# Feed-forward's first product: all of it by Strassen's scheme, in two passes of 768 tokens

## The reference, cut to what matters

```python
def trunk(x, ...):
    mix = token_mixer(rms_norm(x, ln1_pre_g), ...)          # attention and DeltaNet mixers
    x = x + rms_norm(mix, ln1_post_g)
    hid = jnp.square(jax.nn.relu(rms_norm(x, ln2_pre_g) @ w_ff_in))   # (T,1024) @ (1024,4096)
    return x + rms_norm(hid @ w_ff_out, ln2_post_g)
```

## Time and profile before

| | us |
|---|---|
| runs shown (3): median, lowest, highest | 2766.1, 2765.39, 2768.83 |
| the profiled execution, its own time | 2763.01 |
| its span, from the first to the last instruction | 2761.2 |
| PE busy in the span | 2525.7 (91%) |
| `ff_in`, from its first DMA issue to the end of its last product | 1677.2 to 2200.2 |
| the same, from the end of the first pair's part | 1751 to 2200 |

### The profile page before, as it was taken

The page is one execution under the profiler, slowest core; times in us unless marked ns, Lnnn a source line. Parts: engine busy times, 40 slices in busy tenths (PEclk is TensorE's granted clock), DMA queues, the critical chain, the costliest instruction groups (busy, mean ns, idle before and its releaser), DMA issues. The chain is left out here.

```text
span 2761.2 us, 33798 instructions
## 1 busy us (share of the span) xinstructions
PE 2525.7 (91%) x12600; PEld 2106.7 (76%) x12600; DVE 1312.7 (48%) x1700; ACT 890.0 (32%) x1437; POOL 533.8 (19%) x475
## 2 busy tenths in 40 slices
PE   6999999898989979996596993999999889999998
PEld 5888888787979977774485882788888768887887
DVE  5665225256555428886643434644344352234332
ACT  4333323262111117785200332322222141133221
POOL 3352236330111100001420332211121000000000
PEclk9999999999999999998698996999999999999999
DMA  4233212586556551332555444322322273345442
GB/s 136 73 92 88 78 54 102 180 253 215 167 177 186 172 171 70 136 116 74 191 167 180 165 163 150 96 81 88 99 81 85 78 249 112 109 160 201 158 156 103
DMA packets 310734, 373.40 MB, mean 135 GB/s; under 512 B 55760, under 2 KB 237136, under 8 KB 306000
## 3 DMA queue, kind: packets, MB, share of 16 engines
q1 hardware_dynamic: 219712, 294.50, 33.6%
q10 hardware_dynamic: 90896, 77.18, 8.5%
HBM read 251.98 MB, written 119.64 MB: 135 GB/s over the span
## 5 line engine op out<-in xcount | busy, mean ns | idle before, releaser
L2476 PE MATMUL y_ps<-w_hi,hid_hi 128*128 128x512 f32 x768 | 301.1, 392 | 24.4 <-DVE w_lo L2560 16.7
L2476 PE MATMUL y_ps<-w_lo,hid_hi 128*128 128x512 f32 x768 | 300.0, 391 | 0.0
L2476 PE MATMUL y_ps<-w_hi,hid_lo 128*128 128x512 f32 x768 | 299.7, 390 | 0.0
L2566 DVE TENSOR_TENSOR hid_lo<-ff_raw,hid_hi 128x1024 fp32r<-128x1024 f32 x96 | 113.9, 1223 | 319.2 <-ACT hid_hi L2530 319.1
L2530 ACT ACTIVATE hid_hi<-ff_raw 128x1024 fp32r<-128x1024 f32 x96 | 97.3, 1054 | 355.7 <-PE y_ps L2476 329.1
L2117 PE MATMUL ff_ps<-ffx_sums,w_ops 128*128 128x512 f32 x768 | 179.4, 393 | 13.7 <-DVE ffx_sums L2252 13.7
L2476 PEld LDWEIGHTS y_ps<-w_hi,hid_hi 128*128 128x128 f32 x768 | 144.9, 189 | 57.7 <-DVE w_lo L2560 18.2
L2117 PE MATMUL ff_ps<-ffx_rest,w_ops 128*128 128x512 f32 x768 | 181.5, 392 | 8.1 <-DVE ffx_rest L2252 8.1
L2117 PEld LDWEIGHTS ff_ps<-ffx_sums,w_ops 128*128 128x128 f32 x768 | 145.5, 190 | 45.1 <-issue 14.8
L2117 PEld LDWEIGHTS ff_ps<-ffx_rest,w_ops 128*128 128x128 f32 x768 | 145.7, 190 | 38.9 <-issue 8.5
L115 PE MATMUL proj_ps<-ht_hi,win_hi 128*128 128x512 f32 x576 | 173.0, 408 | 0.0
(11 more groups left out here) (255 smaller groups left out, 4885.9 us busy)
## 6 DMA issues: line engine op xcount, KB each, us to landing
ff_raw<-s_hid_s SPq DMA_DIRECT2D x96, 512.0 KB, 4.4
arena<-s_dn_s SPq DMA_DIRECT2D x24, 1024.0 KB, 5.7
s_hid_s<-ff_outs SPq DMA_DIRECT2D x96, 256.0 KB, 2.3
w_raw<-in_w_ff_in SPq DMA_DIRECT2D x16, 1024.0 KB, 5.6
ff_raw<-in_w_ff_out SPq DMA_DIRECT2D x32, 512.0 KB, 4.8
win_raw<-in_w_in SPq DMA_DIRECT2D x27, 512.0 KB, 3.6
s_made_s<-arena SPq DMA_DIRECT2D x12, 1024.0 KB, 4.7
arena<-s_made_s SPq DMA_DIRECT2D x48, 256.0 KB, 6.4
```

Of the source, the lines that this page charges most:

```text
L2476: mm = pe.matmul(acc[:, bank(u, t)], x[:, (t if opens(t) else kh), k], y[:, w], start=w == 0 and first == 0, stop=w == KF - 1 and first == 2)
L2566: dve.tensor_tensor(hlo[:, b, ks].rearrange("p k j -> p (k j)"), raw[:, r], f32(hhi[:, b, ks]).rearrange("p k j -> p (k j)"), ALU.subtract ...
```

## The change

The 1536 tokens are split into two passes of 768, and each pass into two halves of 384 (`WIDE`). In each pass all 16 pairs of weight tiles are gone through, so that there are 32 units (`UNITS`), each of seven products of 12 matmuls with 384 columns; the plain remainder is gone. The weights are loaded, summed and split once for each pass, twice in all. `w1_raw` and `w1_sums` have two buffers each; unit x uses buffer x % 2. All four token sums are made on DVE. C11 is rectified and squared on DVE; C22, C21 and C12 on ACT, in two instructions each.

In `after`, the lines are: loads L2058 (weights) and L2067 (tokens), stores L2085; ACT high parts L2125, token high parts L2135, ReLU L2139, square L2141, copy of P1 L2152; DVE low parts L2168, token low parts L2173, token sums L2183, C11 L2211, its ReLU and square L2214, U2 L2219, U4 L2224, U3 L2228, C22 L2231, C21 L2233, C12 L2238.

```diff
 def ff_in(nc, io):
-        raw = c.sb("w1_raw", [P, KD, 2 * P])
-        sums = c.sb("w1_sums", [P, 4, HK, P])
+    PASSES = 2
+    UNITS = PASSES * PAIRS
+    WIDE = TOK // (2 * PASSES)
+        raw = c.sb("w1_raw", [P, 2, KD, 2 * P])
+        sums = c.sb("w1_sums", [P, 2, 4, HK, P])
...
             @block.sync
+                def load_weights(x):
+                    if x >= 2:
+                        sp.wait_ge(s["w_lo"], 7 * (x - 1))
+                    i = x % PAIRS
+                    sp.dma_start(raw[:, x % 2], ...).then_inc(w_in[x % 2], 16)
...
+                load_weights(0)
+                load_tokens(0)
+                load_weights(1)
+                for x in range(UNITS):
+                    p, i = divmod(x, PAIRS)
+                    if i == 1 and p + 1 < PASSES:
+                        load_tokens(p + 1)
+                    for o in (C11, C22, C21, C12):
+                        if o == C12 and x + 2 < UNITS:
+                            load_weights(x + 2)
+                        if o == C11:
+                            sp.wait_ge(s["curved"], x + 1)
+                        else:
+                            sp.wait_ge(s["squared"], 3 * x + o)
+                        sp.dma_start(io["hid_s"][...], outs[:, o]...).then_inc(out_stored[o], 16)
...
             @block.tensor
+                for x in range(UNITS):
+                    for q in range(7):
+                        if 7 * x + q >= 8:
+                            pe.wait_ge(*used(*divmod(7 * x + q - 8, 7)))
+                        pe.wait_ge(s["w_lo"], 7 * x + q + 1)
+                        if i == 0:
+                            pe.wait_ge(s["x_lo"], 7 * p + q + 1)
...
             @block.scalar
+                for x in range(UNITS):
+                    done(act, x, P1)
+                    act.activation(p1[:], bank(x, P1), ACT.Copy).then_inc(s["p1_done"], 1)
+                    for q in range(7):
+                        if more:
+                            high(x + 1, q)
+                            if i == 0:
+                                prep(p, q)
+                        if q == P7:
+                            relu2(x, C22, "c22_made")
+                            relu2(x, C21, "c21_made")
+                    relu2(x, C12, "c12_made")
...
             @block.vector
+                def following(x, q):
+                    if x + 1 < UNITS:
+                        low(x + 1, q)
+                        if (x + 1) % PAIRS == 0:
+                            prep((x + 1) // PAIRS, q)
...
+                    dve.tensor_tensor(outs[:, C11], p1[:], bank(x, P2), ALU.add).then_inc(s["c11_made"], 1)
+                    following(x, P1)
...
+                    dve.tensor_tensor(outs[:, C21], u2[:], bank(x, P4), ALU.subtract).then_inc(s["c21_made"], 1)
+                    following(x, P4)
+                    following(x, P7)
...
+                    following(x, P3)
+                    if p + 1 < PASSES and i in (4, 6, 8, 10):
+                        token_sum(p + 1, (i - 4) // 2)
```

More of the change, by code:

```diff
@@ L2000, in ff_in @@
     HK = KD // 2
[L2001 to L2005, removed]
+    C11, C22, C21, C12 = range(4)
     with ExitStack() as ctx:
         c = Core(nc, ctx, "ff_in")
[L2008 to L2012, removed]
-        raw = c.sb("w1_raw", [P, KD, 2 * P])
-        w_ops = c.sb("w1_ops", [P, 8, 2, HK, P], F32R)
-        sums = c.sb("w1_sums", [P, 4, HK, P])
[L2016 to L2019, removed]
+        front = c.sb("ffx_raw", [P, 8, HK, WIDE])
+        x_ops = c.sb("ffx_ops", [P, 7, 2, HK, WIDE], F32R)
+        raw = c.sb("w1_raw", [P, 2, KD, 2 * P])
+        w_ops = c.sb("w1_ops", [P, 7, 2, HK, P], F32R)
+        sums = c.sb("w1_sums", [P, 2, 4, HK, P])
+        p1 = c.sb("p1", [P, WIDE])
+        u2 = c.sb("u2", [P, WIDE])
+        u4 = c.sb("u4", [P, WIDE])
+        outs = c.sb("ff_outs", [P, 4, WIDE])
@@ L2067, in prep_views @@
[L2067 to L2075, removed]
+        w_in = [c.sem(f"w_in{u}") for u in range(2)]
@@ new lines, in ff_in, with part_of @@
+        out_stored = [c.sem(f"out_stored{u}") for u in range(4)]
+        r21, r22, r11, r12, t4f, t3f, t1f, t2f = (front[:, n].rearrange("p k t -> p (k t)") for n in range(8))
+        QUADRANT = {0: (0, 0), 1: (1, 0), 2: (0, 1), 3: (1, 1)}
+        SOURCE = {B11: r11, B21: r21, B22: r22, T1: t1f, T2: t2f, T3: t3f, T4: t4f}
+        ARRIVES = {B11: 0, B21: 1, B22: 3}
+        SUMMED = {T1: 0, T2: 1, T3: 2, T4: 3}
+        def part_of(x, op):
+            i, kh = {A11: (0, 0), A12: (0, 1), "A21": (1, 0), A22: (1, 1)}[op]
+            return raw[:, x % 2, kh * HK:(kh + 1) * HK, i * P:(i + 1) * P]
@@ new lines, in _ @@
+                load_weights(0)
+                load_tokens(0)
[9 more added lines that the diff above has]
+                            sp.wait_ge(s["curved"], x + 1)
+                        else:
+                            sp.wait_ge(s["squared"], 3 * x + o)
+                        tile, half = {C11: (0, 0), C22: (1, 1), C21: (1, 0), C12: (0, 1)}[o]
+                        t0 = (p * 2 + half) * WIDE // P
+                        sp.dma_start(io["hid_s"][t0:t0 + WIDE // P, :, 2 * i + tile].rearrange("t p j -> p t j"),
+                                     outs[:, o].rearrange("p (t j) -> p t j", j=P)).then_inc(out_stored[o], 16)
@@ L2112, in _ @@
+                for o in range(4):
+                    sp.wait_ge(out_stored[o], 16 * UNITS)
             @block.tensor
             def _(pe):
[L2115 to L2123, removed]
@@ L2137, in remainder @@
[L2137 to L2140, removed]
-                        for k in range(HK):
[L2142 to L2145, removed]
@@ L2174, in _, with done, out_free, flat @@
+            def done(eng, x, q):
+                eng.wait_ge(s["product"], 7 * x + q + 1)
+            def out_free(eng, x, o):
+                if x:
+                    eng.wait_ge(out_stored[o], 16 * x)
+            def flat(a):
+                return a.rearrange("p k t -> p (k t)")
             @block.scalar
             def _(act):
-                def high(i, op):
-                    operand_ready(act, i, op)
-                    act.activation(w_ops[:, op, 0], source(op), ACT.Copy).then_inc(s["w_hi"], 1)
@@ L2195, in relu2 @@
-                def relu2(i, o, q):
-                    done(act, i, q)
-                    out_free(act, i, o)
-                    dst = outs[:, slot(i, o)]
-                    act.activation(dst, bank(i, q), ACT.Relu).then_inc(s["r_out"], 1)
-                    act.wait_ge(s["r_out"], 2 * i + (o == O_R1) + 1)
-                    act.activation(dst, dst, ACT.Square).then_inc(s["squared"], 1)
-                high(0, A11)
-                for n in range(HK):
-                    prep(n)
-                high(0, A12)
@@ new lines, in prep, with relu2 @@
+                def prep(p, q):
+                    of = RIGHT[q]
+                    if of in ARRIVES:
+                        act.wait_ge(x_in[ARRIVES[of]], 16 * (p + 1))
+                    else:
+                        act.wait_ge(s["t_made"], 4 * p + SUMMED[of] + 1)
+                    if p:
+                        done(act, p * PAIRS - 1, q)
+                    act.activation(flat(x_ops[:, of, 0]), SOURCE[of], ACT.Copy).then_inc(s["x_hi"], 1)
+                def relu2(x, o, made):
+                    act.wait_ge(s[made], x + 1)
+                    act.activation(outs[:, o], outs[:, o], ACT.Relu).then_inc(s["rectified"], 1)
+                    act.wait_ge(s["rectified"], 3 * x + o)
+                    act.activation(outs[:, o], outs[:, o], ACT.Square).then_inc(s["squared"], 1)
@@ new lines, in _ @@
+                for q in range(7):
+                    high(0, q)
+                    prep(0, q)
+                for x in range(UNITS):
+                    p, i = divmod(x + 1, PAIRS)
+                    more = x + 1 < UNITS
+                    done(act, x, P1)
+                    if x:
+                        act.wait_ge(s["u2_done"], x)
+                    act.activation(p1[:], bank(x, P1), ACT.Copy).then_inc(s["p1_done"], 1)
+                    for q in range(7):
+                        if more:
[6 more added lines that the diff above has]
+                    relu2(x, C12, "c12_made")
@@ new lines, in token_sum @@
+                def token_sum(p, n):
+                    dst, a, b, need = ((t1f, r12, r11, (0, 2)), (t2f, r22, t1f, (3,)), (t3f, r22, r12, ()), (t4f, t2f, r21, (1,)))[n]
+                    for m in need:
+                        dve.wait_ge(x_in[m], 16 * (p + 1))
+                    if p:
+                        dve.wait_ge(s["x_lo"], 7 * p)
+                    if n in (1, 3):
+                        dve.wait_ge(s["t_made"], 4 * p + (1 if n == 1 else 2))
+                    dve.tensor_tensor(dst, a, b, ALU.subtract).then_inc(s["t_made"], 1)
@@ new lines, in following @@
+                def following(x, q):
[3 more added lines that the diff above has]
```

(11 more changed lines are left out.)

313 lines of the change are left out of this document (87 added, 226 removed).

## The result

| | before | with the change |
|---|---|---|
| median of 4 runs | 2765.94 us (2765.39 to 2768.83) | 2841.93 us (2836.40 to 2843.77) |
| profiled execution | 2763.0 us | 2842.19 us |
| its span | 2761.2 us | 2840.4 us |
| PE's last product of the stage ends | 2200.2 us | 2275.6 us |

The ratio is 1.0269, with an interval of 1.0251 to 1.0287: 76 us slower, where 50 were forecast. The time is 26 us above the one predicted, inside the range.

What follows compares the result with a forecast made beforehand. A closed ring without PE, 17.1 us a round against PE's 14.56, bounds the stage: 1730 + 496 (29 rounds) + 6.7 + 17.6 ends PE at 2250 against 2200.2, +50 us, so 2816 us; range 2795 to 2850.

Steps and rivals of the forecast that it cites:

- The ring: Closed loop of weights load, DVE and ACT work up to C21's store, next load; without PE, 17.1 us a round.
- landing to C21: From a weights load's landing to the end of C21 on DVE: 9.34 us.
- to C21's square: From the landing through ACT's rectifying and squaring of C22 and C21: 10.94 us.
- to the load's issue: From the landing until SP has issued C21's store and the next load: 11.38 us.
- Issue to landing: Weights load from its issue on SP until it lands: 5.75 us taken, from a range of 5.5 to 6.6.
- My upper bound: Slowest weights landing allowed for, 6.6 us, which makes a round of 18.0 us.
- the beginning: Stage start, DVE the bound on token and weight preparation: load of unit 2 lands at 1730, uncertain by 5 us.
- Narrow matmuls: PE's 384-column matmuls: 0.173 us each forecast; rival had them cost 0.227 like wide ones, +110 us, 2876; 4%.
- The change of pass: One round mid-stage where four low parts of tokens stand ahead of C21 on DVE: 6.7 us longer.
- The rival on the other side: PE stays the bound, the round falling under 14.56 us: PE ends at 2171, 29 us less, 2737; 10%.
- DVE and POOL: Shared SBUF port: POOL gives way by 0.45 us; by the skill's full-block rule the round would be about 17.6.
- The clock: PE's granted clock in the stage: stays 1.00 despite two waits of about 1.2 us a round; nothing charged.

Runs made afterwards that it cites:

- Experiment 1: Changed kernel with the load for unit x+2 issued at the head of unit x's turn on SP, ahead of C11's store: 2737.31 us, 0.9913 of the kernel before.
- experiment 5: Changed kernel with the third of three matmuls per contraction slice (low weights by high tokens) left out in this stage: 2830.69 us.
- experiment 2: Changed kernel with POOL's four sums cut to one column of each 128 from unit 2 on, load left in place: 2746.1 us.
- experiment 3: Changed kernel with the load issued once C21 is squared, ahead of the stores of C22 and C21: 2824.99 us.

## Why the prediction was right, and where a term was off

**The ring was right, link by link.** The prediction's landing to C21 was 9.34, measured 9.39; to C21's square 10.94, measured 11.01; to the load's issue 11.38, measured 11.45. All three were put together from instructions of 512 columns and their spacing. (The text there gives 0.4 for the issue of C21's store, its total holds 0.44, and 0.44 was measured; by the same terms the shortest round is 16.9, not 16.8.) Experiment 1 opens the ring and the loss is gone; experiment 5 takes a third from PE and the loss stays; experiment 2 shortens a link by 3.27 us and the round shortens by as much, until PE's 14.56 us nearly bind.

**The mis-sized term is "Issue to landing".** I took 5.75 us from loads of the kernel before. Over the 30 loads in the ring, for units 2 to 31, it was 6.49 us in the mean, from the issue to POOL's first sum. 0.74 x 29 = 21.5 us. It shows in ACT's waits, too: 4.9 us where up to 4 was forecast. My upper bound, 6.6 with a round of 18.0, came from one row of the same group and was the better choice; the reason that I gave for going above the usual 5.6, the two stores just ahead, is worth only 0.1 to 0.2 us by experiment 3. The links of the chain, 0.07 us each round, add 2 us, the beginning 1.4 (landing of unit 2 at 1731.4, forecast 1730; 1.0 of it is that load's own landing, 6.72 us), the end 0.3: PE ends at 2275.6 instead of 2250.

**The rest, 3.8 us** of the 79.2 by which the spans differ, lies behind the stage. Of it, 3.4 us lie between the first product of `ff_out` and the end of the span (2216.5 to 2761.2 before, 2292.3 to 2840.4 now), in code that the change leaves alone. It was not forecast, and its cause is open.

**Narrow matmuls: right.** In experiment 1 PE has no gap in the second pass:

```profile
1949.63 220.72 PE L2102 MATMUL ff_ps<-ffx_ops,w_ops 128*128 128x384 f32 x1272 [0.41 <-DVE ffx_ops L2173]
```

220.72 / 1272 = 0.1735 us each, where 0.173 was forecast. That rival is out.

**The change of pass: right.** Four low parts of tokens stand in that round. DVE's first of them, which meets POOL, and C21:

```profile
1982.90 2.57 DVE L2173 TENSOR_TENSOR ffx_ops<-ffx_raw,ffx_ops 128x1536 fp32r<-128x1536 f32 x1 [0.17 <-ACT ffx_ops L2135]
...
1996.82 0.55 DVE L2233 TENSOR_TENSOR ff_outs<-u,ff_ps 128x384 f32<-128x384 f32 x1
```

From the landing at 1980.86 to C21's end, 1997.37, it is 16.51 us against 9.39, and the round lasts 24.5 us against 17.85: 6.7 more, as forecast.

**The rival on the other side** asked for a round under 14.56 us. It did not come, but its time did, as soon as the load was moved: 2737, measured 2737.3 in experiment 1. That PE's end was met (2171, measured 2170.3) is the mechanism; that the total was met to 0.3 us is luck, for the 3 us that I added from the profiled execution to the median were 0.2 here, and 4.0 us that I had not counted came in behind the stage (565.0 us from PE's end to the end of the span, 561.0 before). The start of unit 1 in that rival, 1718.6, is given without its working. The rule of the Trainium skill's first page, "Trainium Kernel Development and Optimization", section "Best Practices", that double-buffering overlaps DMA with compute, holds there and fails in the changed kernel, at 2841.9 us, with the same two buffers.

**DVE and POOL.** POOL's three later sums took 1.61, 1.59 and 1.73 us, against 1.27 to 1.30 for the first, which begins before DVE's first low part; so POOL gave way by 0.3 to 0.5 us. The Trainium skill, "SBUF — State Buffer", section "SBUF: two separate sides", would have it wait out a whole DVE instruction, 0.55 to 0.68 us; by that the round would have been 17.6. The round did come near that, but through the landing: the part that the rule speaks of measured 9.39, not the 9.8 that it would make.

**The clock: the term was right, its reason was not.** I charged nothing because I expected the granted clock to stay at 1.00. It fell (below), and cost nothing because PE has 3.3 us to spare in each round.

## What to carry to other kernels

Two buffers hide a load only if its issue point is free of the results of the unit that it should run ahead of: look at what stands ahead of the load in its queue, and follow that back to see whether it leads to the load itself. If it does, walk once round the ring, landing to landing, and compare it with the bound engine's time; no engine's busy share will show it. Take the landing from the slower rows, not from the median of loads that were issued under other conditions.

## What was not expected of the hardware

**Landings.** A load of 1 MB in the same pieces landed 5.6 us after its issue in the kernel before, and 6.4 us in the changed one (medians). Taking stores from ahead of it gave 6.2, a third of PE's work away 6.0, one buffer 6.0, another place in SBUF 6.4, the early issue 6.2 (all medians). No single one of these brings back 5.6, and what does is open. The Trainium skill, "DMA: Bandwidth & Descriptors", section "Measured (HBM→SBUF, 128 partitions, SWDGE, issued from GpSimd)", has 6.15 us for 1 MB on another path, issued from POOL and counted without the issue. The values here, which hold the issue, lie on both sides of it, so this row does not tell which of them is the usual one.

**The granted clock after short waits.** The busy time by stretch for one unit, right behind PE's wait of 2.23 us at 2043.44 and then on:

```profile
2043.40:2047.00 3.60, 3.56 (x12) 3.60 (x13) 3.60 (x4) 1.83 (x4) 3.60 (x3) 0.55 0.18 55
2047.00:2060.00 13.00, 12.84 (x74) 12.52 (x72) 6.69 (x11) 4.41 (x10) 1.20 (x2) 0.99 0.47 126
```

In the first stretch the mean granted clock is 0.55, near the lower level of 1.2 GHz (0.5), although PE had been idle for only 2.23 us; then it is back. Between 1735 and 2276 us there are seven such spells, behind waits of 1.81 to 4.35 us, five of them behind 2.23 or less; a wait of 2.00 us at 2079.44 and one of 1.78 us at 2025.20 have none. The unit took 16.40 us on PE instead of 14.56, but the next landing came 18.00 us after the last, between neighbours of 18.24 and 18.01: PE is outside the ring, and here the slower clock cost nothing.
